# Rotations in place on one engine, and two kinds of statistics at other places

## The reference, cut to what matters

```
cq, ckv, kr, qs, ks, vs = jnp.split(a @ lw['w_in'], SPLIT_POINTS, axis=-1)
q = (rmsnorm(cq, lw['g_qa']) @ lw['w_qb']).reshape(*lead, H_A, NOPE_DIM + ROPE_DIM)
q_nope = rmsnorm(q[..., :NOPE_DIM], lw['g_qn'])
q_rope = rope(rmsnorm(q[..., NOPE_DIM:], lw['g_qr']), pos, MLA_THETA)
latent = rmsnorm(ckv, lw['g_kva'])
k_rope = rope(rmsnorm(kr, lw['g_kr']), pos, MLA_THETA)
qs = partial_rope(rmsnorm(qs.reshape(*lead, H_B, HD_B), lw['g_qs']), pos)
ks = partial_rope(rmsnorm(ks.reshape(*lead, H_B, HD_B), lw['g_ks']), pos)
# rope: concatenate([x1 * cos - x2 * sin, x2 * cos + x1 * sin])
```

## Time and profile before

| | us |
|---|---|
| median of 3 runs | 1088.38 (1088.36 to 1089.26) |
| profiled execution | 1088.96 |
| its span, first to last instruction | 1087.10 |
| TensorE busy in the span | 1049.2 (97%) |
| VectorE busy | 622.6 (57%) |
| ScalarE busy | 461.9 (42%) |
| GpSimd busy | 111.4 (10%) |

### The profile page before, as it was taken

The page is one execution under the profiler, slowest core; times in us unless marked ns, Lnnn a source line. Parts: engine busy times, 40 slices in busy tenths (PEclk is TensorE's granted clock), DMA queues, the critical chain, the costliest instruction groups (busy, mean ns, idle before and its releaser), DMA issues.

```text
span 1087.1 us, 20895 instructions
## 1 busy us (share of the span) xinstructions
PE 1049.2 (97%) x7954; PEld 924.8 (85%) x7954; DVE 622.6 (57%) x1090; ACT 461.9 (42%) x810; POOL 111.4 (10%) x141
## 2 busy tenths in 40 slices
PE   9999399989999999999999999999999999999998
PEld 8997399656577777777659999999999999999998
DVE  5462479786756766666678964434322434344554
ACT  4424133566555665656583343433211222223522
POOL 5411144341000000000001300000000000000000
PEclk9999699999999999999999999999999999999999
DMA  7764442609885888777652356456523654652232
GB/s 273 273 243 148 156 156 83 209 7 345 284 280 173 267 275 263 230 233 260 216 160 59 105 205 211 158 174 231 203 87 135 233 173 154 231 198 85 85 88 92
DMA packets 68591, 202.32 MB, mean 186 GB/s; under 512 B 7425, under 2 KB 40450, under 8 KB 67234
## 3 DMA queue, kind: packets, MB, share of 16 engines
q1 hardware_dynamic: 66338, 131.41, 36.9%
q0 software_dynamic: 2176, 69.90, 18.1%
HBM read 196.20 MB, written 72.13 MB: 247 GB/s over the span
## 4 chain that ended last, share of the span: by engine, by line
PE 80%; issue 8%; DVE 8%; ACT 2%; POOL 1%; DVEq 0%; POOLq 0%; ACTq 0%
PE ps L564 48%; PE ps L1323 15%; PE ps L1421 4%; PE ps L1298 2%; PE ps L1377 1%; PE ps L1311 1%; PE ps L1355 1%; PE ps L1371 1%; PE ps L1274 1%; PE ps L1269 1%; DVE att L1632 1%; POOL big L445 1%; PE ps L1279 1%; PE ps L1128 1%; PE ps L1521 1%
## 5 line engine op out<-in xcount | busy, mean ns | idle before, releaser
L564 PE MATMUL ps<-aHi,wHi 128*128 128x272 f32 x1152 | 241.6, 291 | 9.3 <-DVE wLo L400 9.2
L564 PE MATMUL ps<-aHi,wLo 128*128 128x272 f32 x1152 | 239.3, 289 | 0.0
L564 PE MATMUL ps<-aLo,wHi 128*128 128x272 f32 x1152 | 238.7, 289 | 0.0
L395 ACT ACTIVATE wHi<-ring 128x1024 fp32r<-128x1024 f32 (+3 forms) x102 | 113.4, 1112 | 242.2 <-PE ps L564 215.7
L400 DVE TENSOR_TENSOR wLo<-ring,wHi 128x1024 fp32r<-128x1024 f32 (+3 forms) x102 | 141.5, 1387 | 121.3 <-ACT wHi L395 121.1
L564 PEld LDWEIGHTS ps<-aHi,wHi 128*128 128x128 f32 x1152 | 182.6, 190 | 11.4 <-issue 9.8
L564 PEld LDWEIGHTS ps<-aLo,wHi 128*128 128x128 f32 x1152 | 182.4, 190 | 0.0
L564 PEld LDWEIGHTS ps<-aHi,wLo 128*128 128x128 f32 x1152 | 180.9, 190 | 0.0
L1671 DVE TENSOR_REDUCE ssq<-att 128x8 f32<-128x512 f32 x128 | 87.1, 681 | 76.8 <-ACT att L962 76.8
L962 ACT ACTIVATE att<-ps 128x512 f32<-128x512 f32 x128 | 76.3, 596 | 100.0 <-PE ps L1323 99.4
L1323 PE MATMUL ps<-wkHi,pgHi 128*128 128x512 f32 x256 | 104.2, 407 | 1.5 <-DVE pgLo L1665 1.2
(11 more groups left out here) (284 smaller groups left out, 1518.6 us busy)
## 6 DMA issues: line engine op xcount, KB each, us to landing
out_o_cv<-in_cv POOLq DMA_DIRECT2D x16, 2044.0 KB, 9.8
ring<-in_wgu SPq DMA_DIRECT2D x44, 512.0 KB, 3.7
big<-in_pgt SPq DMA_DIRECT2D x128, 144.0 KB, 2.9
big<-in_pgl SPq DMA_DIRECT2D x128, 128.0 KB, 2.3
kv<-in_ck SPq DMA_DIRECT2D x8, 1792.0 KB, 10.4
ring<-in_win SPq DMA_DIRECT2D x21, 512.0 KB, 3.6
kv<-in_cv SPq DMA_DIRECT2D x8, 1024.0 KB, 5.6
kv<-in_cv SPq DMA_DIRECT2D x24, 256.0 KB, 6.0
```

The costliest lines, as they stand in the source:

```text
L395: nc.scalar.activation(wHi[:, u % 2, 0:width], ring[:, u % 2, 0:width], ACT.Copy).then_inc(w_hi, 1)
L564: ins = nc.tensor.matmul(pair[rows, a, 0:HT], w[:, c], xx[:, k, a * HT:(a + 1) * HT], start=(k == 0 and z == 0), stop=(k == nk - 1 and z = ...
```

## The change

The diff has four parts. A rotation is made by VectorE alone: shuffle, product of the tile with the cosine table in place, product of the partners with the sine table, addition in place; GpSimd's two functions are gone, and its queue holds copies, sums of squares and output transfers only. The statistics of the plain keys stand in steps 13 to 16 in place of 10 to 13, each behind that of a window key, and ScalarE's squares of the plain keys move from tiles 9, 11 and 12 to tiles 11, 12, 14 and 15. The last plain query's statistic stands ahead of the last rotation, which goes behind the first unit's maxima; the last gathering and its roots stand between the first and the second value tile. The low part of the key weights is made in unit 13 in place of unit 7.

```
-        stats += [(g, 0) for g in g_kn + g_ks[:]]
+        stats += [(g, 0) for pair in zip(g_ks, g_kn) for g in pair]
...
-            need = {... P_KEYS: (g_ks[-1], 0), ...}[p]
+            need = {... P_KEYS: (g_kn[-1], 0), ...}[p]
...
-        def pool_cos(g):
-            q = groups[g]
-            nc.gpsimd.wait_ge(n_out, out_no[g])
-            if rope_no[g] > 1:
-                nc.gpsimd.wait_ge(n_rope, rope_no[g] - 1)
-            nc.gpsimd.tensor_tensor(tmp[:, 0, :], q["src"][0], C[:, q["rope"][1]:q["rope"][1] + T],
-                                    ALU.mult).then_inc(n_nc, 1)
-        def pool_rope(g):
-            nc.gpsimd.wait_ge(n_nc, rope_no[g])
-            nc.gpsimd.wait_ge(n_rr, rope_no[g])
-            nc.gpsimd.tensor_tensor(groups[g]["src"][0], tmp[:, 0, :], tmp[:, 1, :], ALU.add).then_inc(n_rope, 1)
...
             nc.vector.stream_shuffle(tmp[:, 1, :], q["src"][0], q["rope"][0]).then_inc(n_rot, 1)
             nc.vector.wait_ge(n_rot, i)
+            nc.vector.tensor_tensor(q["src"][0], q["src"][0], C[:, q["rope"][1]:q["rope"][1] + T], ALU.mult).then_inc(n_nc, 1)
             nc.vector.tensor_tensor(tmp[:, 1, :], tmp[:, 1, :], C[:, q["rope"][2]:q["rope"][2] + T],
                                     ALU.mult).then_inc(n_rr, 1)
+            nc.vector.wait_ge(n_nc, i)
+            nc.vector.wait_ge(n_rr, i)
+            nc.vector.tensor_tensor(q["src"][0], q["src"][0], tmp[:, 1, :], ALU.add).then_inc(n_rope, 1)
...
             for k in range(8):
                 pool.wait_ge(w_used, min(2 * k + 4, 9 + k))
                 copy_k(k // 2, k % 2)
-                if k == 3:
-                    pool.wait_ge(s_c2, 16)
-                    pool_heads(g_kr)
-                if k in (4, 5, 6, 7):
-                    pool_heads(g_qs[k - 4])
-            pool_add_cq(0)
-            pool_add_cq(1)
-            for i, g in enumerate(g_ks):
-                pool_cos(g)
-                pool_add_cq(2 + i)
-                pool_rope(g)
-            pool_heads(*g_qr)
+            for i in range(KQ):
+                pool_add_cq(i)
...
-            act_post = {... 9: (two_keys(0), key_square(0), key_square(1)), ...
-                        11: (new_keys(), key_square(2)), 12: (two_vs(0), key_square(3)), ...
+            act_post = {... 9: two_keys(0), ...
+                        11: (new_keys(), key_square(0)), 12: (two_vs(0), key_square(1)), ...
+                        14: (vs_copy(4), key_square(2)), 15: (new_key_root(), key_square(3)), ...
...
             value_copy(0)
+            head_root(P_QN)
             value_copy(1)
-            head_root(P_QN)
...
                     values_of(0)
+                    gather(P_QN)
                     values_of(1)
-                    gather(P_QN)
...
-                         10: [(dve_rope, g_qs[0]), (dve_scale, g_qs[1]), (dve_stat, g_kn[0])],
-                         11: [(dve_rope, g_qs[1]), (dve_scale, g_qs[2]), (dve_stat, g_kn[1])],
-                         12: [(dve_rope, g_qs[2]), (dve_scale, g_qs[3]), (dve_stat, g_kn[2])],
-                         13: [(dve_rope, g_qs[3]), (dve_stat, g_kn[3]), (dve_stat, g_ks[0])],
-                         14: [(dve_stat, g_ks[1]), (new_key_sums,)], 15: [(dve_stat, g_ks[2])], 16: [(dve_stat, g_ks[3]), (new_key_recip,)],
+                         10: [(dve_rope, g_qs[0]), (dve_scale, g_qs[1])],
+                         11: [(dve_rope, g_qs[1]), (dve_scale, g_qs[2])],
+                         12: [(dve_rope, g_qs[2]), (dve_scale, g_qs[3])],
+                         13: [(dve_rope, g_qs[3]), (dve_stat, g_ks[0]), (dve_stat, g_kn[0])],
+                         14: [(dve_stat, g_ks[1]), (dve_stat, g_kn[1]), (new_key_sums,)], 15: [(dve_stat, g_ks[2]), (dve_stat, g_kn[2])],
+                         16: [(dve_stat, g_ks[3]), (dve_stat, g_kn[3]), (new_key_recip,)],
...
-            dve_rope(g_qr[1])
+            dve_stat(g_qn[-1])
...
                 if n == 0:
-                    dve_stat(g_qn[-1])
+                    dve_rope(g_qr[1])
...
-                if n == 7:
+                if n == 13:
                     v.wait_ge(wk_hi, 1)
                     v.tensor_tensor(wkLo[:, :, :], wK[:, :, :], wkHi[:, :, :].bitcast(F32), ALU.subtract).then_inc(wk_lo, 1)
```

More of the change, by code:

```diff
@@ L403, in gather @@
         def gather(p):
-            need = {P_IN: (g_qs[-1], 0), P_KEYS: (g_ks[-1], 0), P_QR: (g_qr[-1], 0), P_QN: (g_qn[-1], 0)}[p]
+            need = {P_IN: (g_qs[-1], 0), P_KEYS: (g_kn[-1], 0), P_QR: (g_qr[-1], 0), P_QN: (g_qn[-1], 0)}[p]
             nc.tensor.wait_ge(n_st, stat_no(need))
@@ L744, in _ @@
                 pool.tensor_tensor(xs[:, :], xs[:, :], tmp[:, k % 2, :], ALU.add).then_inc(x_acc, 1)
-            def pool_heads(*heads):
-                for g in heads:
-                    pool_cos(g)
-                    pool_rope(g)
             for k in range(8):
@@ L869, in two_vs @@
                 vs_copy(t + 1)
-            act_post = {5: x_root, 7: lambda: head_root(P_IN), 9: lambda: (two_keys(0), key_square(0), key_square(1)), 10: lambda: two_keys(2),
-                        11: lambda: (new_keys(), key_square(2)), 12: lambda: (two_vs(0), key_square(3)), 13: lambda: two_vs(2),
-                        14: lambda: vs_copy(4), 15: new_key_root, 16: lambda: head_root(P_KEYS)}
+            act_post = {5: x_root, 7: lambda: head_root(P_IN), 9: lambda: two_keys(0), 10: lambda: two_keys(2),
+                        11: lambda: (new_keys(), key_square(0)), 12: lambda: (two_vs(0), key_square(1)), 13: lambda: two_vs(2),
+                        14: lambda: (vs_copy(4), key_square(2)), 15: lambda: (new_key_root(), key_square(3)), 16: lambda: head_root(P_KEYS)}
             in_dst = {D_KR: [U_KR], D_LAT: [U_LAT, U_LAT + 1], D_VS: [U_VS + i for i in range(HP)],
```

## The result

The changed kernel took 1074.72 us in the median (1073.41 to 1075.33, three executions) against 1088.38; the ratio is 0.987 with an interval of 0.9847 to 0.9892. It is faster, as forecast, but by 13.7 us and not by 20.0, and 0.7 above the range. The profiled execution took 1075.33 (span 1073.5), its mean granted clock is 0.995; that of before was 1088.96 at 0.990.

The account below looks back on a forecast made before the run. TensorE was taken as the bound nearly everywhere except between 107.7 and 133.0. Saved 21.6 - 1.6 - 0.45 + 0.4 = 20.0 from 1088.96, giving 1069.0 us; forecast 1067.5 to 1071 (0.62), range 1066 to 1074.

Parts of the forecast that it names:

- The prize: Tiles 13 to 15: TensorE regains 18.01 us of waits and 3.60 of low clock behind the holes, together 21.6.
- the ring: GpSimd's rotation stands behind a copy awaiting a later tile; VectorE's next shuffle waits, coming weights behind it; TensorE lacks them.
- The gathering after tile 16: The moved plain-key statistics end at 147.75, the gathering started at 147.29: TensorE waits 0.45 us.
- the start of attention: Work goes behind the last plain statistic and the gathering ahead of the second value tile: +0.45 us (-1.3 to +2.8).
- The -0.4 for the low key weights: Moved from where VectorE is the later engine to where it idles: 0.4 us gained (bounds -1.2 and +0.6).
- Tiles 17 to 23: VectorE's own pace makes TensorE late by 0.45 + 0.3 + 0.9 = 1.6 us (bounds 0.4 and 4.5).
- Net +0.47 per step: Steps 18 to 20: a rotation adds 1.41 us on VectorE, less 2 x 0.47 of GpSimd contention coming back.
- rival 1: Port contention: VectorE meets each of five query squares (1.36 us) in full, 4.5 later, 1073.5; chance 0.13.
- The granted clock fell only behind holes of over 8 us: Later waits of 1.28 and 2.46 us left the clock at 1.00 over the stretch to 240.
- Rival 4: Tiles 17 to 23: VectorE becomes the bound, with holes long enough for the low clock; slower, 1093.7 us; chance 0.03.
- Rivals 2 and 3: Besides rival 2, rival 3: ScalarE's square still holds the value copies, the second hole stays, 1077.9 us; chance 0.05.
- rival 2: Weights late: two copies beside one transfer, one or two tiles 3 us late, 1073 to 1075; chance 0.07.

Follow-up runs that it names:

- x2: Kernel before, GpSimd's share of each rotation queued ahead of the cache copy instead of behind it, nothing changed on VectorE: 1075.89 us.
- y7: Changed kernel with short fillings (unread products where TensorE waits), low part of the key weights back at unit 7: 1071.25 us.
- z1: Changed kernel, unfilled, GpSimd's two memsets and the copies behind them held back until unit 14's probabilities are scaled: 1081.30 us.
- y6: Changed kernel with short fillings (unread products where TensorE waits), last plain query's statistic, its gathering and root put back: 1074.17 us.
- v1: y4 with the plain keys' statistics and squares back at tiles 10 to 13: 1067.51 us.
- y4: Changed kernel with four rotations of tiles 18 to 21 shared with GpSimd, plus short fillings (unread products where TensorE waits): 1069.10 us.
- x1: Changed kernel with GpSimd's two long memsets cut into eight pieces each: 1076.80 us.
- y5: Changed kernel with short fillings (unread products where TensorE waits), plain keys' statistics and squares back at tiles 10 to 13: 1070.60 us.
- x3: Changed kernel, unfilled, with the four rotations of tiles 18 to 21 shared with GpSimd as before: 1074.70 us.
- x10: Kernel before with GpSimd's share of each rotation ahead of the cache copy, plus long fillings (unread products where TensorE waits): 1075.73 us.

## Why the prediction was wrong, point by point

**The prize was right.** 21.6 forecast, 21.8 measured, and x2 shows by the ring alone that its cause was right too: with no other change 18.8 came back in its profile, and the wait that x2 leaves holds 2.0 of the rest.

**The gathering after tile 16 was right** (0.45 forecast, 0.39 of waiting), and so was the start of attention: +0.45 forecast, 18.3 to 17.9 measured. The -0.4 for the low key weights agrees in size (17.9 to 18.3), but y7 doesn't show it in the time, and most of the wait it was to shorten was the memsets' (2.01 in the changed kernel, 0.77 in z1). What the early statistic is worth, y6 shows: some 1.7.

**Tiles 17 to 23, the size was wrong.** 1.6 forecast, 3.2 measured (21.5 to 18.3); the waits alone are 0.39 + 1.08 + 0.46 + 0.62 = 2.55. The step was "Net +0.47 per step". The distances of the shuffles are 7.06, 6.29 and 6.88, on average 6.74 against 5.90, so +0.84. The product and the addition cost what was forecast (2.9 for the rotation from 69.34 to 72.26), but of GpSimd's contention 0.57 came back and not 0.94. One query square per tile is enough to hold VectorE: the pass at 140.10 takes 1.62 and that at 152.04 1.71, against 0.79 and 0.72 alone. Both end 0.6 behind GpSimd's pass, as the row of before did, though rival 1's full 1.36 was met by none. The move of the statistics, priced only by its 0.45 at tile 16, is part of the lag: without it v1 is 0.9 ahead of y4 behind tile 23.

The Trainium skill ("SBUF — State Buffer", section "SBUF: two separate sides") puts such waits down to an exclusive lock held for an instruction, and the rows near 140 and 152 agree. Those of x1 go further: VectorE's scaling lasted beyond not one memset but a whole row of them.

**"The granted clock fell only behind holes of over 8 us" was the step that failed.** It rested on one profiled execution, in which waits of 1.28, 2.46 and 2.22 left the clock at 1.00, and the sum had no term for them. Rival 4 named the mechanism but put its point near 8 us and its place in tiles 17 to 23. Behind the same two places the changed kernel lost 2.95 (18.3 to 15.3) and 1.2 (15.0 to 13.8), the second more than 300 us after anything that was changed. Without these 4.15 and the 1.6 of lag the profiled 1075.33 would be 1069.6. Filling gives back 3.6 of it in the median.

**Signs.** As named: no wait over 1 between tiles 12 and 15, the clock at 1.00 from 100 to 140, no shuffle waiting for GpSimd, the gatherings at 0.39 and 0.62. Attention's first maxima came 17.8 earlier (203.6 to 185.8), where about 20 was named. Of the signs of being wrong, waits over 3 in tiles 17 to 23 were not reached (2.55, with tile 16's), but what was gained by 200 was in part lost again by 304: 3.0 of 18.3, at the fall near 215. That sign pointed at the step that failed. Rivals 2 and 3: one weight came 0.73 late at 168, the 3 us of rival 2 are in single executions of x1 and y5 only; no hole remained.

**What stays open.** Why a wait of 2 us is followed by the low clock in one execution and not in another, and why it was the rule after the change and rarer before. Nor is it known why a weight transfer is 3 to 4 us late in some executions of one kernel and not in others.

## What to carry to other kernels

Before moving work off an engine, look at what stands ahead of it in that engine's queue: here two lines in another order gave what the whole change gave (medians of 1075.89 and 1075.04). A wait of about 2 us on TensorE is a risk to its clock even if the trace at hand shows none; price it, or fill it with products shorter than the wait, measured first. What is put ahead of a queue's DMAs delays them too, and here the loss showed some 60 us later.

## What was not expected of the hardware

The granted clock fell to its lower level behind waits of 1.74 (x3), 1.96 (x10), 2.01 and 2.22 (changed), 2.28 (y6) and 2.60 us (x1), and stayed at the upper one behind others of 1.73 (changed), 1.97 and 2.45 (x2), 2.13 (y5), 2.22 and 2.46 (before), most of them the same places in other executions. The stretches shown behind them, 3.5 to 8.4 us at a mean clock of 0.51 to 0.59, cost 1.0 to 3.0 where that was measured. Sixteen memsets of 0.15 us in a row held one scaling on VectorE for 2.19; two of 0.94 held a pair of them for 1.87, where the pair takes 0.62 without memsets.
